# A fused two-block transformer kernel: VectorE's share of the first layer's item loop put in another order

## The reference, cut to what matters

```python
def gmlp_mixer(u, v, v_norm_g, ws, bs):
    u = gelu(u); v = rms_norm(gelu(v), v_norm_g)          # 4 head groups of 128 channels
    mixed = einsum('gts,bnsgc->bntgc', tril(ws), v) + bs
    return u * mixed

def rglru_mixer(gate_in, x_in, conv_w, conv_b, wa, ba, wx, bx, lam):
    xc = conv_b + sum(xp[:, k:k + S] * conv_w[k] for k in range(4))   # causal convolution, width 4
    r = sigmoid(xc @ wa + ba); i = sigmoid(xc @ wx + bx)              # block diagonal
    log_a = -8.0 * r * softplus(-lam)
    a = exp(log_a); b = sqrt(-expm1(2.0 * log_a)) * (i * xc)
    h = scan(h = a * h + b)
    return gelu(gate_in) * h

def nsa_mixer(q, kv, ...):     # 8 heads x 3 kinds (compressed, selected, window), softmax in each
    hid = gelu(einsum('cbgnf,cgfe->cbgne', blocks_of_keys_and_values, cmp_w1)) ...

gates = sigmoid(mg)                                       # (tokens, 4 branches, 1024)
merged = sum(gates * branch, axis=2); return merged @ w_out
```

## Time and profile before

| | |
|---|---|
| median of 3 runs | 1885.22 us |
| the profiled execution's own time | 1885.83 us |
| its span (first to last instruction) | 1884.0 us |
| TensorE busy | 1829.6 us (97%) |
| VectorE busy | 1176.7 us (62%) |
| ScalarE busy | 887.3 us (47%) |
| mean granted TensorE clock | 0.988 of full |
| the items | about 115 to 327 us of the span |

### The profile page before, as it was taken

How to read it: one execution, slowest core, us unless ns; L and a number is a source line. 1 busy time by engine, 2 the same in 40 slices (tenths; PEclk the granted TensorE clock), 3 DMA queues, 4 the chain that set the end, 5 groups by cost and what they waited for, 6 DMA issues and landing times.

```text
span 1884.0 us, 25827 instructions
## 1 busy us (share of the span) xinstructions
PE 1829.6 (97%) x10816; PEld 1568.6 (83%) x10816; DVE 1176.7 (62%) x1458; ACT 887.3 (47%) x1091; POOL 49.9 (3%) x107
## 2 busy tenths in 40 slices
PE   7999999999999999999999999999999999999998
PEld 7998889878888887788888898888788889887887
DVE  5345666479898898645468966554645456745454
ACT  4433442367777675544323245444444345535442
POOL 0030000000000000000000000000000010000000
PEclk9989999999999999999999999999999999999999
DMA  8342334479899888555333007544555534226540
GB/s 353 135 157 90 113 112 180 174 291 363 329 351 343 340 338 323 186 193 201 134 116 131 25 3 294 195 177 182 203 190 176 191 135 152 96 98 248 187 176 39
DMA packets 51523, 363.58 MB, mean 193 GB/s; under 512 B 5712, under 2 KB 5840, under 8 KB 8784
## 3 DMA queue, kind: packets, MB, share of 16 engines
q1 hardware_dynamic: 51264, 359.83, 51.3%
q10 hardware_dynamic: 144, 2.10, 0.3%
HBM read 360.86 MB, written 1.05 MB: 192 GB/s over the span
## 4 chain that ended last, share of the span: by engine, by line
PE 87%; DVE 7%; ACT 4%; issue 2%; POOL 0%; DMA 0%; DVEq 0%; SPq 0%; POOLq 0%; ACTq 0%
PE bank L2633 8%; PE bank L2635 8%; PE bank L2634 8%; PE bank L2171 7%; PE bank L2660 4%; PE bank L2658 4%; PE bank L2659 4%; PE bank L2225 4%; PE bank L2525 3%; PE bank L2527 3%; PE bank L2526 3%; PE bank L2210 3%; PE bank L2448 3%; PE bank L2356 3%; PE bank L2540 2%
## 5 line engine op out<-in xcount | busy, mean ns | idle before, releaser
L1305 DVE TENSOR_TENSOR w_a<-ring,w_a 128x2048 fp32r<-128x2048 f32 x221 | 504.2, 2290 | 277.2 <-ACT w_a L814 276.3
L814 ACT ACTIVATE w_a<-ring 128x2048 fp32r<-128x2048 f32 x221 | 420.2, 1912 | 188.2 <-PE bank L2660 90.1
L2633 PE MATMUL bank<-w_a,h 128*128 128x512 f32 x536 | 212.7, 397 | 6.0 <-DVE h L1369 6.0
L2635 PE MATMUL bank<-w_a,h 128*128 128x512 f32 x536 | 209.2, 390 | 0.0
L2634 PE MATMUL bank<-w_a,h 128*128 128x512 f32 x536 | 208.7, 389 | 0.0
L1305 DVE TENSOR_TENSOR w_b<-ring,w_b 128x2048 fp32r<-128x2048 f32 x62 | 142.0, 2291 | 67.8 <-ACT w_b L814 67.1
L2171 PE MATMUL bank<-h,w_a 128*128 128x256 f32 x1088 | 145.8, 289 | 0.7 <-DVE w_a L1305 0.7
L2171 PEld LDWEIGHTS bank<-h,w_a 128*128 128x128 f32 x1088 | 137.8, 196 | 3.5 <-issue 3.2
L814 ACT ACTIVATE w_b<-ring 128x2048 fp32r<-128x2048 f32 x62 | 118.6, 1914 | 45.7 <-PE bank L2660 25.7
L1077 ACT ACTIVATE sil<-bank,tiny 128x256 f32<-128x256 f32 x88 | 41.8, 475 | 175.2 <-PE bank L2635 175.2
L2633 PEld LDWEIGHTS bank<-w_a,h 128*128 128x128 f32 x536 | 100.7, 188 | 27.1 <-DVE h L1369 4.9
(11 more groups left out here) (473 smaller groups left out, 3277.1 us busy)
## 6 DMA issues: line engine op xcount, KB each, us to landing
ring<-in_stream SPq DMA_DIRECT2D x330, 1024.0 KB, 4.9
G<-in_gains SPq DMA_DIRECT2D x15, 512.0 KB, 5.7
cmp_area<-in_cmp_w ACTq DMA_DIRECT2D x1, 2048.0 KB, 10.9
sm<-in_small SPq DMA_DIRECT2D x1, 1582.0 KB, 13.1
con<-in_consts SPq DMA_DIRECT2D x1, 1032.0 KB, 17.1
X<-in_x SPq DMA_DIRECT2D x2, 512.0 KB, 4.9
out_x<-X SPq DMA_DIRECT2D x4, 256.0 KB, 2.0
sm<-in_small SPq DMA_DIRECT2D x1, 730.5 KB, 23.5
```

Source lines behind the costliest of these rows:

```text
L814: act.activation(w_slot(unit)[:, 0, :], ring[:, unit % RING, :], ACT.Copy).then_inc(S("w_hi"), 1)
L1305: dve.tensor_tensor(w_slot(unit)[:, 1, :], ring[:, unit % RING, :], w_slot(unit)[:, 0, :].bitcast(FP32), ALU.subtract).then_inc(S("w_lo"), 1)
L2633: pe.matmul(bank[4 + t][:, :], x_hi, w[0][:, k, :], start=first, stop=False)
L2635: ins = pe.matmul(bank[4 + t][:, :], x_lo, w[0][:, k, :], start=False, stop=end)
```

## The change: the diff, and what stands where

Nothing is computed differently. Four things move.

1. `schedule` gets an argument `ahead`. ACT keeps 3 (`GATE_W - 1`). DVE calls with 2 (`GATE_W - 2`) and makes 2 subtractions before the loop, not 3. So each subtraction stands one gate item later than its copy.
2. The second gmlp pair is an item earlier on both engines: PE at items 2 and 3, DVE at items 1 and 2.
3. `lam_2` goes from item 7 to item 15.
4. `conv(m)` goes in two halves: the first two of its four operations at an odd item, the other two at the next. Items 7 to 14 have one half each.

```diff
-        def schedule(run_slot, run_item, gate_split=lambda m: None):
+        def schedule(run_slot, run_item, gate_split=lambda m: None, ahead=GATE_W - 1):
             for i in range(len(ITEMS)):
-                if i in MG_ITEMS and MG_ITEMS.index(i) + GATE_W - 1 < len(MG_ITEMS):
-                    gate_split(MG_ITEMS.index(i) + GATE_W - 1)
+                if i in MG_ITEMS and MG_ITEMS.index(i) + ahead < len(MG_ITEMS):
+                    gate_split(MG_ITEMS.index(i) + ahead)
...
-            for m in range(GATE_W - 1):          # DVE, ahead of the loop
+            for m in range(GATE_W - 2):
                 gate_split(m)
...
-            def conv(m):
+            def conv(m, half):
                 w = P1("conv_w")
-                link(dve.tensor_scalar(xc[:, m, :], rec[:, m, 0:T], ...))
-                for k in range(1, CONV_A):
+                if half == 0:
+                    link(dve.tensor_scalar(xc[:, m, :], rec[:, m, 0:T], ...))
+                for k in ((1,), range(2, CONV_A))[half]:
...
-                ins.then_inc(S("xc"), 1)
+                if half == 1:
+                    ins.then_inc(S("xc"), 1)
...
-                if i in (1, 3):                  # DVE
-                    gmlp(i // 2)
+                if i in (1, 2):
+                    gmlp(i - 1)
-                if i == 7:
+                if i == 15:
                     lam_2()
-                if i in (7, 9, 11, 13):
-                    conv((i - 7) // 2)
+                if 7 <= i < 7 + 2 * MT:
+                    conv((i - 7) // 2, (i - 7) % 2)
...
-            schedule(run_slot, run_item, gate_split)
+            schedule(run_slot, run_item, gate_split, GATE_W - 2)
...
-                if i in (2, 4):                  # PE
-                    gmlp(i // 2 - 1)
+                if i in (2, 3):
+                    gmlp(i - 2)
```

More of the change, by code:

```diff
@@ L1500, in soft_2 @@
                 ins.then_inc(S("p_ok"), 1)
-            def conv(m):
+            def conv(m, half):
                 w = P1("conv_w")
-                link(dve.tensor_scalar(xc[:, m, :], rec[:, m, 0:T], w[:, m:m + 1], P1("conv_b")[:, m:m + 1],
-                                       ALU.mult, ALU.add))
-                for k in range(1, CONV_A):
+                if half == 0:
+                    link(dve.tensor_scalar(xc[:, m, :], rec[:, m, 0:T], w[:, m:m + 1], P1("conv_b")[:, m:m + 1],
+                                           ALU.mult, ALU.add))
+                for k in ((1,), range(2, CONV_A))[half]:
                     ins = dve.scalar_tensor_tensor(xc[:, m, :], rec[:, m, k:k + T], w[:, MT * k + m:MT * k + m + 1],
```

## The result

The changed kernel takes 1870.18 us (median of 5 runs, 1867.42 to 1875.16) against 1885.26 before. The ratio is 0.991 with a 95% interval of 0.9889 to 0.993: 13 to 21 us faster, 17 at the middle of the ratio and 15.1 by the medians. The forecast was 1875.2 with a range from 1870.5; the direction and the places were right, the size was not.

What follows compares the result with a forecast made beforehand. PE, busy 97% of the span, was taken to bound the kernel, so only its waits and clock could give time: 1.4 + 7.7 - 0.7 + 2.2 = 10.6 us off 1885.8 gives 1875.2 us, range 1870.5 to 1880.3.

Steps and rivals of the forecast that it cites:

- What bounds the kernel: PE, busy 97% of the span; the change can act only through PE's waits, 10.1 us, and its clock.
- Part 1: Second gmlp pair and compression: compression starts at 129.4, a new wait of 0.9 to 1.0 us, gain 1.4 us.
- Part 2: Moving lam_2 and halving the convolution frees 3.0 us on DVE at item 7, covering PE's 2.56 us wait; no cost.
- the 2.56: PE's wait in us for DVE at the scores around item 7, claimed to go through the work moved off that item.
- Part 3: Subtractions an item behind copies: all 7.7 us of softmax-chain waits go (with Part 2), less 0.7 for the last subtraction.
- Part 4: Clock at the compression: first 2.9 us at full speed gain 2.9, longer tail costs 0.7, net 2.2 us gained.
- a longer tail: Low clock after the compression's narrow rows, taken as 4.2 us long, costing 0.7 us more than before.
- The last term: End of the gate loop: PE waits about 0.7 us for half 31's subtraction, behind one more recurrence step; loss 0.7.
- the second: Rival: softmax chain stays late, waits only change name, 5.1 us stay, time 1880.3 us; chance 0.10.
- the first: Rival: the clock at the compression gives nothing, time 1877.4, or 1878.8 us with the longer tail; chance 0.20.
- the rule: Rival: the clock never falls while PE issues back to back, compression 6.9 us, time 1869.1 us; chance 0.06.
- the slower case: Rival: PE waits for subtractions at halves 16 to 31, costing 19.7 us, time 1894.9 us; chance 0.03.

Runs made afterwards that it cites:

- gmlp_only: Kernel before with only the second gmlp pair an item earlier on PE and VectorE; 1882.03 us, ratio 0.9985.
- after_two_subs: Changed kernel with the subtraction of half 2 back ahead of the loop and that of half 31 ahead of the third recurrence step; 1871.19 us, ratio 0.9925.
- sub_only: Kernel before with only VectorE's subtractions an item behind ScalarE's copies; 1878.04 us, ratio 0.9962.
- lamconv_only: Kernel before with only the recurrence constants at item 15 and the convolution by halves; 1882.97 us, ratio 0.9988.
- after: The changed kernel in its first measurement, against the kernel before; median 1870.18 us, profiled execution 1872.21 us, ratio 0.991.
- after_again: The changed kernel measured once more, unaltered, on another chip; 1871.37 us, ratio 0.9931 to the kernel before.
- the two gates24 kernels: gates24_spread and gates24_two_subs, changed kernels with the 24-column attention gate products placed between wide ones; 1874.46 and 1870.26 us.
- gates24_two_subs: Changed kernel with the attention gates' 24-column products spread between wide ones and the subtractions of halves 2 and 31 back in place; 1870.26 us, ratio 0.9935.
- spread: Changed kernel with the compression's 32 products spread between wide products of gate halves 1 to 4, in another PSUM bank; 1862.90 us, ratio 0.9889.
- spread_two_subs: Changed kernel with the compression spread between wide products and the subtractions of halves 2 and 31 back in place; 1861.61 us, ratio 0.988.
- combined: Changed kernel with the compression and the attention gates' products both spread and the subtractions of halves 2 and 31 back; 1862.73 us, ratio 0.9893.
- gates24_spread: Changed kernel with the 24-column attention gate products placed one by one between wide products of the next projection; 1874.46 us, ratio 0.9947.

## Why the prediction was wrong in size

**What bounds the kernel.** Right. All of the 13.6 us came from PE's waits and its clock between 120 and 300 us, and nothing behind it took them back.

**Part 1.** Right to 0.1 us: start at 129.30 against 129.4. The one new wait came in another form. I had PE waiting 0.9 to 1.0 for the bank at the second gmlp pair. Instead half 2 starts 0.7 late (122.30, where the rows give 120.65 + 0.92), since its subtraction now stands in item 0, and the pair another 0.2 to 0.3 late (125.45 against 122.30 + 2.88), too short for a row of the waits. Together that is the forecast 0.9 to 1.0. In gmlp_only, where the subtractions stand as before, it is a single wait of 0.80. One cause stood behind both, the two subtractions ahead of DVE's first gmlp pair: after_two_subs took one away, and both waits went.

**Part 2.** Right as far as the changed kernel goes, wrong on its own. The 3.0 us taken from item 7 did not have to cover the 2.56: sub_only lost that wait without them. By itself (lamconv_only) the part moves the waits on and gives 0.5. Item 15 was no trouble.

**Part 3, the first step that failed.** The mechanism was right and all 7.7 us went. But I took the waits view's figure for what a wait costs, and called the sum of these figures the most that removed waits can give. The loop became 8.9 us shorter although the new wait for half 31 came on top, which costs 0.8 (after_two_subs, without it, has a loop of 129.72, not 130.50). So the eight waits that the view gives as 7.7 had cost 9.7, 0.2 to 0.25 us more each. The rows show where: in after, PE's 8 products before a transpose without a wait are

```profile
252.06 1.12 PE L2173 MATMUL bank<-h,w_a 128*128 128x256 f32 x8
253.02 0.49 PE L2409 MATMUL bank<-con,arena 128*128 128x128 f32 x3
253.26 1.20 PE L2173 MATMUL bank<-h,w_a 128*128 128x256 f32 x8
```

and in the kernel before, with the wait,

```profile
263.89 1.12 PE L2171 MATMUL bank<-h,w_a 128*128 128x256 f32 x8
265.64 0.55 PE L2407 MATMUL bank<-con,arena 128*128 128x128 f32 x3 [0.64 <-DVE arena L1499]
265.95 1.19 PE L2171 MATMUL bank<-h,w_a 128*128 128x256 f32 x8
```

From the first product to the half behind it: 1.20 against 2.06 us, so the wait cost 0.86, where its row says 0.64. The row counts from the products' modelled end (263.89 + 1.12 = 265.01), but the next instruction starts 0.96 after the group's start when nothing holds it; that is 0.16. The other 0.06 is the slower restart (0.31 against 0.24 to the next half). The last term, 0.7 for the subtraction of half 31, was right in mechanism and size: its row says 0.53, its cost by the loops is 0.8.

**Part 4, the second step that failed.** The model was right: no fall until the narrow products have run for a while, a fall in their midst without any pause, a longer tail. Its size was taken from a single event (2.9 us, at 99.6). Without a pause ahead of the compression it was 4.6 us in after, 4.3 in gmlp_only, 3.7 in after_two_subs and 3.0 in after_again, and 4.1 and 4.8 in the two gates24 kernels. Their compressions took 9.3, 9.6, 10.1, 10.8, 9.8 and 9.1 us, against 10.8 forecast (13.7 - 2.9), so the forecast stood at the slow end of what occurs. The tail cost 1.1 in after and not 0.7.

The net gain, 4.34 - 1.07 = 3.3 us against 2.2, was mis-sized through the sum of two lengths, that of narrow products at full speed (the head) and that of low clock behind them (the tail). after_again had the forecast's compression (10.75 us) and then a tail of 2.5 us, not 4.2; after had the longer head (4.6) and a tail of 5.5. I had modelled the tail as a length of its own behind the narrow rows; what was alike is the whole low stretch, 10.2 us from fall to rise in five of the six profiles without a pause (6.8 in gates24_two_subs), where the forecast's low part of the compression and its tail make 7.9 + 4.2 = 12.1. From the start of the compression to the first branch product these five take 25.6 to 25.7 us, wherever the clock fell; the four with a pause, at half speed for 13.7 or 17.1 us, take 27.4 or 28.8 to 28.9. Nor does the fall come at a certain time behind the first narrow product. In the ten profiles with the compression in one piece it begins anywhere from 126.4 to 131.3 us, but the fall lies at 130.4 to 131.3 in six and at 133.5 to 134.0 in four.

**The rule of the Trainium skill** (TensorE: Matmul & The Clock Gate, section "What's actually happening"). The prediction's plain reading of it, that a PE that issues without a pause stays at full speed, fails here. The trace of after has no wait row of PE from 122.30 to the fall at 133.9. Only the three kernels where wide products lie between the compression's narrow ones (spread, spread_two_subs, combined) kept the clock.

**The sum and the range.** Both misses have the same sign: 1.9 us in the loop and 1.1 in the clock, 3.0 of the 13.7 us. The profiled execution, 1872.2, is still within the range; the median of the five executions lies another 2.0 below it, and that took the result out. I had called this difference slack, on the ground that the clock varies from run to run. It does, and the profile is one of the draws. The five executions of the changed kernel:

| span, us | 1865.6 | 1867.0 | 1868.4 | 1870.4 | 1873.4 |
|---|---|---|---|---|---|
| mean granted clock | 0.993 | 0.993 | 0.991 | 0.989 | 0.987 |

The time follows the clock, and the profiled run is the second slowest. The low end of the range, 1870.5, should have allowed for this draw; it would have held the result with 1 us more.

**The rivals.** None of them came. The waits did not change name (against the second), the clock gave 3.3 us net (against the first), it still fell (against the rule), and PE waited for subtractions at two places for 0.5 us each, not at sixteen (against the slower case).

**Open.** The low stretches of the routing, 330 to 390 us, differ between profiles of kernels that do the same there (none in sub_only, 17.1 us in gates24_spread). Whether an earlier end of the gate halves makes them shorter, or each profile only draws them, was not separated, and it is a part of the two or three us by which the medians move against the profiles. How long narrow products keep full speed (2.3 to 4.8 us in the eight profiles in which the clock fell in their midst) and why a pause of PE brought the clock down in some profiles and not in others were not traced to a cause either.

## What to carry to other kernels

When an engine's program alternates long-latency producers and a serial chain, put each consumer one round behind its producer: here 19 of 21 waits for a copy that had just been issued vanished when VectorE's lead was made one shorter, and that was most of the gain. A wait row counts from a modelled end of the matmul before it; the cost is the distance between starts, compared with the same piece without a wait. Here 32 products of 36 columns in a row brought TensorE's clock down in all six profiles in which nothing paused PE ahead of them; mixed one by one between wide ones, they did not in any of three, and that was worth more than half of the whole change. And one profiled execution is one draw of the clock: a gain of a few microseconds is read from several executions.

## What was not expected of the hardware

- Narrow products kept full speed for 3.0 us (24 columns, before) and for 3.0 to 4.8 us (36 columns, six profiles without a pause ahead of them) before the fall. The low stretch that began under the 24 columns lasted 6.8 us in the kernel before (99.7 to 106.5) and 3.4 in after_again (100.1 to 103.6), with the same instructions around it.
- A PE wait of 2.56 us cost no clock in the kernel before and 3.4 us of half speed in gmlp_only, in the same place of the program. The pause ahead of the compression ended with the clock down in the kernel before (2.37 us) and with full speed in sub_only (2.02 us).
- 32 narrow products mixed into four gate halves (96 wide products), at 0.46 us for one narrow and two wide, kept the granted clock at 1.00.
